# Inverse roots on Pool instead of ACT and DVE, outside the expert rows of a two-block transformer kernel

## The reference

```
# block 1
h  = rms_norm(x, g1) * (1 + scale1) + shift1          # scale, shift, gate from silu(c) @ w_ada
qa, ka, va, qb, kb, vb = split(h @ w_in)
mixed = [rms_norm(windowed_gqa(qa, ka, va)), rms_norm(neighbourhood_attention(qb, kb, vb))]
x  = x + gate1 * (mixed @ w_out)
h2 = rms_norm(x, g2) * (1 + scale2) + shift2
# per token: 8 heads x 16 experts chosen by keys; u, v are rows of two tables
x  = x + gate2 * sum_k gelu(h2 . u[idx_k]) * g_k * v[idx_k]
x  = rms_norm(x, final_g)
# block 2
qkv = rms_norm(x, attn_g) @ w_in_2 ;  heads of q and k are rms-normed, then rotated
a = gqa(qa, ka, va) ;  b = rms_norm(differential_attention(qb, kb, vb, lam)) * (1 - lambda_init)
x = x + [a, b] @ w_out_2
x = x + relu(rms_norm(x, mlp_g) @ w_up)**2 @ w_down
```

## Time and profile before

| | |
|---|---|
| median of 3 runs | 2314.7 us (2314.51 to 2316.34) |
| the profiled execution, its time | 2320.89 us |
| the profiled execution, its span | 2319.1 us |
| mean granted TensorE clock | 0.970 |
| busy: PE, DVE, ACT, Pool | 2093.2, 1317.7, 921.0, 930.9 us |
| expert rows, transfers of software queue | 536.90 MB |

### The profile page before, as it was taken

One profiled execution on the slowest core, in us unless ns is written; L12 is line 12 of the kernel. 1 busy time (PEld: TensorE's weight loads), 2 busy tenths in 40 slices (PEclk: granted clock), 3 DMA queues, 4 the chain that ended last, 5 costly groups with the idle time before them and its releaser, 6 DMA issues. The chain is left out here.

```text
span 2319.1 us, 21783 instructions
## 1 busy us (share of the span) xinstructions
PE 2093.2 (90%) x6824; PEld 1152.0 (50%) x6824; DVE 1317.7 (57%) x3041; ACT 921.0 (40%) x2340; POOL 930.9 (40%) x585
## 2 busy tenths in 40 slices
PE   7899998898898999888689999999988998999999
PEld 5687543333343333333233333333345554888887
DVE  6133446777778777787564466465446553433432
ACT  2454533444445444444233344344334442321321
POOL 0685004566555666656257766666600000000000
PEclk9899899999999999999899999999998998999999
DMA  8442427999999999999999999999911002232231
GB/s 346 173 146 83 172 109 314 419 421 413 416 413 406 420 418 404 419 419 411 418 418 407 422 420 416 418 422 419 411 58 56 1 0 82 82 109 91 91 109 55
DMA packets 118069, 650.95 MB, mean 281 GB/s; under 512 B 10920, under 2 KB 29376, under 8 KB 46144
## 3 DMA queue, kind: packets, MB, share of 16 engines
q0 software_dynamic: 73728, 536.90, 56.1%
q1 hardware_dynamic: 41280, 107.32, 12.9%
q10 hardware_dynamic: 2944, 5.33, 0.6%
HBM read 647.41 MB, written 2.10 MB: 280 GB/s over the span
## 5 line engine op out<-in xcount | busy, mean ns | idle before, releaser
L859 PE MATMUL bank<-ring,diag 128*128 128x512 f32 x2048 | 994.5, 613 | 148.1 <-ACT diag L1380 146.4
L558 POOL DMA_INDIRECT ring<-in_uv,idx x512 | 799.5, 1562 | 668.9 <-PE bank L859 235.8
L1991 DVE CUSTOM_DVE_ANT_0 zjunk<-ring,h 128x1024 bf16<-128x1024 f32 x512 | 627.3, 1225 | 418.8 <-DMA ring<-in_uv,idx 417.4
L859 PEld LDWEIGHTS bank<-ring,diag 128*128 128x128 f32 x2048 | 368.8, 191 | 708.8 <-ACT diag L1380 423.4
L1374 ACT ACTIVATE zg<-z 128x1 f32<-128x1 f32 x512 | 103.5, 202 | 694.9 <-DVE z L1991 694.3
L1380 ACT ACTIVATE diag<-ident,weight 128x128 f32<-128x128 f32 x512 | 205.5, 401 | 16.8
L823 PE MATMUL bank<-w_inb,hTb 128*128 128x512 f32 (+1 forms) x320 | 146.5, 558 | 0.0
L2177 DVE TENSOR_TENSOR ml_lo<-mlp_raw,ml_hi 128x2048 fp32r<-128x2048 f32 x32 | 73.4, 2293 | 114.4 <-ACT ml_hi L1517 114.4
L790 PE MATMUL bank<-w_q,h2T 128*128 128x512 f32 x256 | 130.2, 600 | 3.6 <-ACT h2T L1269 3.6
L1517 ACT ACTIVATE ml_hi<-mlp_raw 128x2048 fp32r<-128x2048 f32 x32 | 61.1, 1908 | 121.8 <-PE bank L578 107.6
L576 PE MATMUL bank<-hTm_hi,ml_hi 128*128 128x512 f32 x256 | 100.9, 394 | 1.6 <-DVE hTm_lo L2172 1.6
(11 more groups left out here) (250 smaller groups left out, 2632.9 us busy)
## 6 DMA issues: line engine op xcount, KB each, us to landing
ada_w<-in_w_ada SPq DMA_DIRECT2D x24, 1024.0 KB
mlp_raw<-in_w_up SPq DMA_DIRECT2D x16, 1024.0 KB, 5.5
mlp_raw<-in_w_down SPq DMA_DIRECT2D x16, 1024.0 KB, 5.0
win_raw<-in_w_in SPq DMA_DIRECT2D x9, 1024.0 KB, 6.0
w_inb<-in_w_in SPq DMA_DIRECT2D x8, 1152.0 KB, 26.2
w_q<-in_w_query SPq DMA_DIRECT2D x8, 1024.0 KB, 8.7
ring<-in_uv,idx POOLq DMA_INDIRECT x512, 9.8
x<-in_x SPq DMA_DIRECT2D x8, 512.0 KB, 12.7
```

The lines of the kernel that those rows point to most:

```text
L558: e.indirect_dma_start(ring[n % RING], None, a["uv"], bass.IndirectOffsetOnAxis(ap=idx[i][:, j:j + 1], axis=0)).then_inc(s[f"d_ring{n % RI ...
L859: t = e.matmul(bank[2 * (i % 2) + half], diag[n % 4], ring[n % RING][:, 1024 + 512 * half:1536 + 512 * half], start=(j == 0), stop=(j == 127))
L1991: e.tensor_tensor_reduce(out=zjunk, in0=ring[n % RING][:, 0:1024], in1=h2[:, i, :], scale=1.0, scalar=0.0, op0=ALU.mult, op1=ALU.add, accu ...
```

## The change

Pool makes 20 inverse roots, each by two instructions in place (`inverse_root`): a `tensor_scalar` that scales the sum of squares and adds eps, and a `tensor_tensor` with the operation `pow` and a constant -0.5. What goes is ACT's `Sqrt`, DVE's `reciprocal`, and in two kinds of place a DVE `tensor_scalar` by a constant, which is folded into the scale. The roots of `after_gather` for tiles 0 to 2 and of the first seven groups of heads stay on ACT and DVE. The roots on Pool are, in the order of its queue (`ROOTS`): the first norm's (4 columns) at the very head of the queue; behind `win_low(8)` the attention outputs' (4, 1, 1 and 2 columns) and those of `h2`, tile by tile (1 column each); then all 512 rows; then tile 3's two, the last queries' (16 columns), and for each tile the one of `sub_norm2` (4 columns) and the one of the MLP's norm (1 column).

```diff
-NAMES: a_ro, v_r1, v_ro
+NAMES: g_root
+ROOTS = ("first", "o0", "o4", "o5", "x0", "x1", "o6", "x2", "x3", "given", "normed", "queries",
+         "d0", "n0", "d1", "n1", "d2", "d3", "n2", "n3")
+def rooted(name):
+    return 2 * ROOTS.index(name) + 2
...
 @block.gpsimd
+            def inverse_root(name, part, scale, added):
+                e.tensor_scalar(part, part, scale, added, ALU.mult, ALU.add).then_inc(s["g_root"], 1)
+                q.wait_ge(s["g_root"], rooted(name) - 1)
+                e.tensor_tensor(part, part, neg_half.to_broadcast([128, part.shape[1]]), ALU.pow).then_inc(s["g_root"], 1)
+            def root_x(i):
+                q.wait_ge(s["a_ss2"], i + 1)
+                inverse_root(f"x{i}", ss2[:, i:i + 1], 1.0 / D, EPS)
+            q.wait_ge(s["v_const"], 3)
+            q.wait_ge(s["a_ss1"], 4)
+            inverse_root("first", ss1, 1.0 / D, EPS)
             win_low(0)
...
             win_low(8)
+            root_o(0, 4)
+            root_o(4, 5)
+            root_o(5, 6)
+            root_x(0)
+            root_x(1)
+            root_o(6, 8)
+            root_x(2)
+            root_x(3)
             for n in range(512):
                 if n == 4:
-                    q.wait_ge(s["v_h2"], 12)
+                    q.wait_ge(s["v_h2"], 8)
...
+            for step, name in enumerate(("given", "normed")):
+                q.wait_ge(s["v_ag"], 12 * 3 + 7 + 2 * step)
+                inverse_root(name, stats[:, 19 + 4 * step:20 + 4 * step], 1.0 / D, EPS)
+            q.wait_ge(s["v_hs"], 8)
+            inverse_root("queries", rr[:, 3, 0:16], 1.0, 64 * EPS)
             for i in range(3):
+                root_heads(i)
                 sub_norm(i)
+                if i == 2:
+                    root_heads(3)
+                root_last(i)
+            root_last(3)
...
 @block.scalar, the roots outside the rows
-            e.activation(ss1, ss1, ACT.Sqrt, bias=eps, scale=1.0 / D).then_inc(s["a_ss1"], 1)
-                e.activation(part, part, ACT.Sqrt, bias=eps, scale=1.0 / 512).then_inc(s["a_ro"], 1)
-                e.activation(ss2[:, i:i + 1], ss2[:, i:i + 1], ACT.Sqrt, bias=eps, scale=1.0 / D).then_inc(s["a_ss2"], 1)
-                e.activation(ss_b[:, i, :], ss_b[:, i, :], ACT.Sqrt, bias=eps, scale=1.0 / 128).then_inc(s["a_sn"], 1)
-                e.activation(ss3[:, i:i + 1], ss3[:, i:i + 1], ACT.Sqrt, bias=eps, scale=1.0 / D).then_inc(s["a_n3"], 1)
-                head_root(7, rr[:, 3, 0:16])
+                    if i == 3: return            # after_gather, tile 3
...
 @block.vector, their inverses
-            e.reciprocal(ss1, ss1).then_inc(s["v_r1"], 1)
-                e.reciprocal(part, part).then_inc(s["v_ro"], 1)
-                e.reciprocal(ss2[:, i:i + 1], ss2[:, i:i + 1]).then_inc(s["v_h2"], 1)
+                q.wait_ge(s["g_root"], rooted(f"x{i}"))
-                e.reciprocal(sb, sb).then_inc(s["v_sn"], 1)
-                e.tensor_scalar(sb, sb, 1.0 - LAMBDA_INIT, None, ALU.mult).then_inc(s["v_sn"], 1)
-                e.reciprocal(ss3[:, i:i + 1], ss3[:, i:i + 1]).then_inc(s["v_n3"], 1)
+                q.wait_ge(s["g_root"], rooted(f"n{i}"))
-                head_scales(5, 7, rr[:, 3, 0:16])
```

More of the change, by code:

```diff
@@ L336, in block_program @@
         one = small("one", 128)
-        eps = small("eps", 1)
+        eps, neg_half = small("eps", 1), small("neg_half", 1)
         c_col, c_tmp = small("c_col", 8), small("c_tmp", 8)
@@ L1317, in _ @@
             sums(7)
-            root(6, 8)
-            root_x(1)
             stream = chain(choose(), *[project2(i) for i in range(3)])
@@ L1462, in sub_norm2 @@
                 q.wait_ge(s["v_rot"], 48)
[L1463 removed]
+                q.wait_ge(s["v_sn"], i)
                 e.activation(sqb, o2[i][:, 512:1024], ACT.Square).then_inc(s["a_sn"], 1)
[L1465 to L1469 removed]
+                for _ in range(7):
                     yield
@@ L1495, in last_queries @@
                 yield
-                yield
-                head_root(7, rr[:, 3, 0:16])
-                for _ in range(7):
+                for _ in range(8):
                     yield
@@ L1908, in after_gather @@
                     yield
-                    q.wait_ge(s["a_ag"], 2 * i + step + 1)
-                    e.reciprocal(ss, ss).then_inc(s["v_ag"], 1)
-                    q.wait_ge(s["v_ag"], c + 2)
+                    if i < 3:
+                        q.wait_ge(s["a_ag"], 2 * i + step + 1)
+                        e.reciprocal(ss, ss).then_inc(s["v_ag"], 1)
+                        c += 1
+                        q.wait_ge(s["v_ag"], c + 1)
+                    else:
+                        q.wait_ge(s["g_root"], rooted("normed" if step else "given"))
                     if step == 0:
                         e.scalar_tensor_tensor(x[:, i, :], x[:, i, :], ssf, slot[2], ALU.mult, ALU.mult).then_inc(s["v_ag"], 1)
-                        q.wait_ge(s["v_ag"], c + 3)
+                        q.wait_ge(s["v_ag"], c + 2)
                     else:
@@ L1935, in head_norm @@
                 qk = rqk[i].rearrange("p (h d) -> p h d", d=64)
-                q.wait_ge(s["v_rr"], SCALED2[n])
+                if n < 7:
+                    q.wait_ge(s["v_rr"], SCALED2[n])
+                else:
+                    q.wait_ge(s["g_root"], rooted("queries"))
                 e.tensor_tensor(qk[:, lo:hi, :], qk[:, lo:hi, :], rr[:, i, lo:hi].unsqueeze(2).to_broadcast([128, hi - lo, 64]),
```

77 lines of the change are left out of this document (30 added, 47 removed).

## The result

The changed kernel takes 2304.1 us (median of 5 runs, 2300.8 to 2306.1), the kernel before 2316.3 in the runs beside them: a ratio of 0.9944, 95% interval 0.9929 to 0.9958. The forecast was 2304.6, within 2299 to 2318. A second group of runs gave 2301.0 and 0.9937 (0.9922 to 0.9952). ACT is busy for 879.9 us, 41 less; Pool for 956.1, 25 more.

The account below looks back on a forecast made before the run. Limits taken: PE to about 354 us, transfers while expert rows arrive, the PE/DVE/ACT ping-pong in block 2, then PE in the MLP. -10.1 + 7.05 - 5.75 - 1.7 + 0.4 = -10.1 us from 2314.7 gave 2304.6, range 2299 to 2318.

Parts of the forecast that it names:

- (a): First root, ahead of the rows: even a slow power is covered by 10 us of other work; nothing gained.
- (b): Root at unit 36: without table switches PE's 2.63 us wait and the half clock behind it go; 8.4 us gained.
- (c): Roots at 311.62 us, ahead of the `h2T` copy: the copy moves up and PE waits less; 1.7 us gained.
- The cap of 8.4: At unit 48: its bias transfer, queued behind query weights, arrives only 8.4 us earlier, limiting the gain from unit 36.
- (d): Tile 3's root ahead of all 512 rows in Pool's queue: row 4 leaves 7.05 us later, passed on whole.
- (e): Tile 3's two roots after the rows: some 1.7 us shorter, but PE goes straight on; nothing gained.
- (f): Units of block 2, after the rows: removed table switches give PE back its waits; 5.75 us gained.
- (g): After the rows, clock regained behind one PE wait of 1.62 us: 1.7 us gained, nothing for later falls.
- (h): Last root, before the MLP: nothing hides it and it takes 0.94 us in place of 0.54; 0.4 us lost.
- clock falls anyway: Rival, chance 0.23: near unit 36 the clock drops even without the wait, gaining 2.6 us, not 8.4; total 2310.4 us.
- little is given back: Rival, chance 0.13: clock dips and DVE's order absorb gains after the rows, and the clock falls too; 2316 us.
- `pow` is slow: Rival, chance 0.14: a one-column power on Pool takes 4.6 us, delaying the rows and last root; +7.7, 2322 us.

Follow-up runs that it names:

- experiment 3: The changed kernel with the root of unit 36 and the reciprocal at unit 38 back on ACT and DVE; 2311.3 us, ratio 0.9972.
- Experiment 4: The changed kernel with tile 3's root in Pool's queue behind the first four expert rows instead of ahead of row 0; 2293.4 us, ratio 0.99.
- experiment 8: The changed kernel with the three roots between the last row and block 2's units back on ACT and DVE; 2303.8 us, ratio 0.9946.
- Experiment 5: The changed kernel plus an unread ACT square root, with its table loads, at seven places behind the rows; 2314.4 us, ratio 0.9987.
- d: The changed kernel with the four roots of the heads' sums back on ACT and DVE; 2310.0 us, ratio 0.9968.
- n: The changed kernel with the four roots of the last norms back on ACT and DVE; 2310.3 us, ratio 0.9973.
- experiment 2: The kernel before with only the nine roots ahead of the rows moved to Pool; 2315.3 us, ratio 0.9995.
- 1: The kernel before with only the roots behind the rows moved to Pool; 2300.9 us, ratio 0.9935.
- Experiment 9: The changed kernel with an extra unread 24-column power on Pool ahead of each of the twenty roots; 2331.3 us, ratio 1.0069.

## Why the prediction was right, and where not

**The power** of one column was sized right (0.548 for 0.5). That was a choice between 0.165 and 4.6 with nothing in the trace to decide it, so the nearness is in part luck; that it grows with the columns was not foreseen. With it the root was right: at the end, the square's last instruction is over at 1945.22 and `norm3` starts at 1946.16, the 0.94 us of the forecast. Pool's first power of four columns starts 0.08 us behind the instruction ahead of it and takes 1.02 us, the later ones 1.01 and 1.02. The Trainium skill (GPSIMD Engine Reference, section Instruction dispatch) has about 6 us at the first call of freshly loaded code; no such time shows here at the first power.

**(a)** is right: DVE's first product starts at 35.60 us in after and at 35.57 in before.

**(b)** was right in its mechanism: the clock is not low because the matmuls are small but behind the wait, and it stays up without it. After has neither the wait nor the 0.50, and experiment 3 brings both back. The size was off. From the keys to the first query (b) and (c) give 6.6 us (83.7 to 77.0) and not 10.1, and three errors can be read apart:

- "Three pairs: 3 x (6.07 - 3.41) = 8.0 us, and with the wait some 10.6" counts too much. The three pairs and the wait take 18.9 us in before (233.95 to 252.88) and not 3 x 6.07 + 2.63 = 20.8, for the first of them began at full clock; in after the three take 10.4 (233.50 to 243.91). That is 8.5 us. The cap of 8.4 hid this error.
- The cap itself was too hopeful: from the keys the bias is there 6.3 us earlier than in before (24.3 for 30.6), not 8.4. This is 2.1 us.
- The prediction took no loss of clock for the wait of PE that its own cap implies. From the bias to the first query it is 52.8 us in after and 53.1 in before, though **(c)** shortens PE's wait by its 1.8; so some 1.5 us are lost, where the granted clock is 0.66 over 5 us.

The last two make up the 3.5 us between 10.1 and 6.6. The rest of the -7.1 in the table, 0.4 us, was there before the root: over all profiled executions the keys leave anywhere between 227.5 and 231.8. The first row's issue, forecast for 0 to 1 us before 354, came at 356.84 for the same reason.

**(d)** is right. From the first query to the first row it is 49.5 us, where 49.8 was worked out, and to row 4 63.1, where 62.3 was. Experiment 4 shows that it was the place in Pool's queue: with the root behind the first four rows, row 4 leaves even earlier than in before.

**(e)**, nothing from tile 3's two roots, stands untested but for experiment 8, which can't tell its three roots from nothing.

**(f) and (g)** failed in size, and the failing step is (g). PE's idle time behind the rows fell by 4.2 us (29.2 to 25.0), near the 5.35 of (f) and (h). But the clock was counted at one place, with 1.7 us, and "for the falls further on I take nothing", while PE's matmuls there got 5.4 to 12.6 us shorter (239.0 or 246.2 to 233.6). The prediction gave that case 0.03. Experiment 5 names the switches as the cause of most of the gain: brought back alone, without any inverse that hangs on them, they cost 10.9 us.

How these split between idle time and clock is not shown as well. The profiled executions of 5 and of the two parts d and n show the idle time of PE (29.7, 27.4 and 28.2 us for 25.0) but not the clock: it is 0.93 as in after, and the matmuls take 234.8, 233.3 and 233.5 us. So an execution with switches need not have the low clock; the 0.89 and 0.92 rest on one execution each, of before and of experiment 2, and these differ by 7 us in the same work. The mean clock over the whole of every timed execution says a little more: its median is 0.972 in before (0.967 to 0.976), 0.976 in both 2 and 5 (0.973 to 0.978), and 0.979 in the changed kernel (0.975 to 0.980). It is lower with the switches, if not in every execution. Which falls of the clock these are stays open.

**The rival "clock falls anyway"** fell with experiment 3; **"little is given back"** with 1; **"`pow` is slow"** with the form row. Experiment 9 shows that its danger was real, but it was priced too low: + 7.7 us against before at 4.6 us for a power, where 15 were measured at 4.76. Its threshold came out about right because a steeper price (7.2 us for each us of the power) starts from a larger gain. The total came out so near because two errors went opposite ways: 5.3 us too hopeful in front of the last row, 9.8 too careful behind it. The 4.5 that are left over, and 0.2 at the end, are the -14.8 of the profiles against the -10.1 forecast; in the medians it is -12.3, since the profiled execution of before stood 4.6 us above its median and that of after 2.0. Part of the nearness of 2304.1 to 2304.6 is that the median of before, too, was 1.6 us higher beside the result than the one that the forecast was taken from.

## What to carry to other kernels

Count a function table's switch by what stands behind it: 2.6 us of loads at unit 36 cost some 7 us, since PE's clock fell to half behind the wait that they made; so look in the trace for every fall of the clock behind a wait that an edit removes, not for the first alone. When work moves to an engine whose queue also issues transfers, place it by what must leave first: one root ahead of the rows instead of behind four of them cost 8 to 11 us. And when a stall goes, look at what is queued for the moment after it: moving eight small loads ahead of a large one gave 4.4 us more (2293.4 to 2289.0).

## What was not expected of the hardware

A power on Pool is paid by the column (0.157 us), so 16 columns are nearly three times as long as four. Small instructions of Pool can stretch beside DVE: the root of two columns at 306.70 took 1.29 us for its `tensor_scalar`, beside a product of DVE from 306.65 to 307.93, and 1.68 for its power, beside the next one. In experiment 9 that `tensor_scalar` again took 1.29 us beside the same product, the extra power behind it 5.15 for its usual 4.16, and the power of two columns, with DVE idle, 0.697. The reverse is larger: DVE's product of 1024 columns takes 1.28 us, and 5.53 at 38.06, while Pool makes its first 2048 columns of `win_lo` (37.42 to 42.5); so it is before, too. In the second execution of the changed kernel it is the neighbouring product, which starts at 37.66 beside a `win_lo` of 37.42 to 42.0, that takes 5.41 us. The Trainium skill (SBUF — State Buffer, section SBUF: two separate sides) states that a GpSimd instruction and a DVE instruction with two SBUF inputs take turns on a shared pair of ports for a whole instruction; these rows agree with it, and a root placed on Pool beside such work pays it too.
